# Prompt attention of a hybrid decoder in 64*64 products: query halves, key halves and identity products in place of transposes

## What is computed

```python
s_c = einsum('btgjd,bcgd->btgjc', qg, kc) - slopes * c_dist    # 63 compressed keys
p_c = masked_softmax(s_c, c_mask); o_c = einsum('btgjc,bcgd->btgjd', p_c, vc)
...  # selected: every causal block (16 of 16 are chosen); window: the last 512 keys
o = g[:, :, 0] * o_c + g[:, :, 1] * o_s + g[:, :, 2] * o_w
```

## Time and profile before

| | us |
|---|---|
| median of three runs (1698.94 to 1709.0) | 1705.83 |
| the profiled execution, its own time | 1709.87 |
| its span, first to last instruction | 1707.8 |
| PE busy over the span | 1625.1 (95%) |
| DVE, ACT, POOL busy | 874.4, 576.3, 411.4 |
| the stage `attend_prompt`: first score to last gate | 678.5 to 923.5 |
| product instructions of the stage: scores, turns, values | 512, 592, 1184 |

### The profile page before, as it was taken

How to read it: one execution, slowest core, us unless ns; L and a number is a source line. 1 busy time by engine, 2 the same in 40 slices (tenths; PEclk the granted TensorE clock), 3 DMA queues, 4 the chain that set the end, 5 groups by cost and what they waited for, 6 DMA issues and landing times. The chain is left out here.

```text
span 1707.8 us, 45233 instructions
## 1 busy us (share of the span) xinstructions
PE 1625.1 (95%) x19863; PEld 1163.6 (68%) x19863; DVE 874.4 (51%) x1780; ACT 576.3 (34%) x1239; POOL 411.4 (24%) x455
## 2 busy tenths in 40 slices
PE   7999999999999998999997989899999999999997
PEld 5788777777776555676666879665678888445443
DVE  3433555556654376777766644361141465634434
ACT  5221444444542113667663211213222211101344
POOL 0212322233331161556454210123100022100110
PEclk9999999999999999999999989899999999999999
DMA  5112010000101305802003975558601220700001
GB/s 165 37 50 56 4 28 17 16 17 16 29 16 35 93 23 117 229 40 100 1 2 106 319 221 175 170 126 190 149 21 50 80 103 16 272 0 1 25 25 50
DMA packets 116872, 136.15 MB, mean 80 GB/s; under 512 B 48620, under 2 KB 99509, under 8 KB 111726
## 3 DMA queue, kind: packets, MB, share of 16 engines
q1 hardware_dynamic: 107426, 83.97, 17.3%
q0 software_dynamic: 9216, 49.29, 9.6%
q10 hardware_dynamic: 36, 0.01, 0.0%
HBM read 120.64 MB, written 16.62 MB: 80 GB/s over the span
## 5 line engine op out<-in xcount | busy, mean ns | idle before, releaser
L1232 PE MATMUL ps<-xnT,rw_side_w 64*64 64x344 f32 x2304 | 213.6, 455 | 3.7 <-ACT zT L1557 1.9
L2672 PE MATMUL ps<-xnT,zT 128*128 128x344 f32 x384 | 121.5, 466 | 0.0
L1232 PEld LDWEIGHTS ps<-xnT,rw_side_w 64*64 64x64 f32 x2304 | 96.1, 133 | 34.6 <-issue 11.7
L2405 POOL TENSOR_SCALAR probs<-probs,row_sums,gates 128x63 f32<-128x63 f32 (+6 forms) x148 | 95.1, 658 | 100.9 <-DVE row_sums L2361 100.3
L2672 PEld LDWEIGHTS ps<-xnT,zT 128*128 128x128 f32 x384 | 72.0, 195 | 36.4 <-issue 6.3
L2310 ACT ACTIVATE probs<-probs,neg_max 128x63 f32<-128x63 f32 (+6 forms) x148 | 87.5, 595 | 1.6 <-DVE neg_max L2351 1.6
L2257 PE MATMUL ps<-kT,zT 64*128 64x512 f32 (+3 forms) x384 | 74.1, 498 | 2.3 <-PEq L82 1.4
L3379 POOL TENSOR_TENSOR mT<-mT,gate_n 128x258 f32<-128x258 f32 x28 | 23.7, 854 | 216.3 <-DVE gate_n L3342 216.3
L2284 PE MATMUL ps<-probsT,kvtok 128*64 128x128 f32 x1056 | 75.3, 280 | 0.0
L2326 ACT ACTIVATE probsT<-ps 128x512 f32<-128x512 f32 (+1 forms) x80 | 45.8, 573 | 82.3 <-PE ps L2270 82.3
L2270 PE MATMUL ps<-ident,probs 128*128 128x128 f32 (+1 forms) x460 | 68.1, 279 | 4.7 <-DVE probsT L2382 3.1
(11 more groups left out here) (623 smaller groups left out, 3613.7 us busy)
## 6 DMA issues: line engine op xcount, KB each, us to landing
w_z<-in_w_in_dram SPq DMA_DIRECT2D x13, 512.0 KB, 5.2
xnT_kept<-xnT SPq DMA_DIRECT2D x1, 4128.0 KB
x_tok<-in_x_prompt_dram SPq DMA_DIRECT2D x8, 512.0 KB
rw_side_w<-in_w_in_dram SPq DMA_DIRECT2D x16, 256.0 KB, 3.5
zT<-in_w_in_dram SPq DMA_DIRECT2D x8, 512.0 KB, 5.0
ring_k<-in_w_in_dram SPq DMA_DIRECT2D x8, 512.0 KB, 5.2
w_out<-in_w_out_dram SPq DMA_DIRECT2D x1, 4096.0 KB
h_tok<-in_x_prompt_dram SPq DMA_DIRECT2D x8, 512.0 KB, 8.6
```

Source lines behind the costliest of these rows:

```text
L1232: last = nc.tensor.matmul(k.ps[half(f), bank, 0:CG], w.side[half(e), g // 3 % 2, c, half(f)], k.xnT[half(e), c, third(g)], start=(phase == ...
L2405: nc.gpsimd.tensor_scalar(every, every, ls[:, at:at + 1], k.gates[:, i, gate:gate + 1], ALU.mult, ALU.mult).then_inc(scaled, 1)
L2672: ins = self.nc.tensor.matmul(self.k.ps[:, self.banks[n % nb], 0:CG], self.w[:, t % 2, c, :], self.k.xnT[:, c, g * CG:(g + 1) * CG], start ...
```

## The change

- Scores: each product for 128 queries becomes two for 64 queries, on the two halves of the partitions of the same bank.
- Turns: a transpose becomes four products of 64*64 with the 64*64 identity (two for the 63 compressed keys). The query half e goes to bank 4 + e, the key half f to half of the partitions. T now stands for a *group* of two pieces (84 groups, 8 of them with one piece), which fills both banks; ACT copies bank 4 and DVE bank 5, after the whole group. Turns of group u wait for both copies of group u-1, values for both copies of their group.
- Values: each product over 128 keys becomes two over 64 keys, with their sums in bank 6 and bank 7.
- The end of a unit: DVE's gate becomes `join`, which adds bank 6 and bank 7 into SBUF (a ring of four); POOL multiplies by the gate (`gated`), three units later in its order. The first values of a unit wait for the join of the unit before.
- The order: where the first of two pieces of values is a unit's last, the second one goes behind the turns, if there are any.

The core of the diff; removed lines that are printed above are left out:

```diff
@@ -2070 +2070,2 @@
-AT_RING, AT_LEAD, AT_GROUP, AT_SLOTS = 6912, 4, 4, 5
+AT_RING, AT_LEAD, AT_GROUP, AT_SLOTS = 6912, 4, 4, 3
+AT_SUMS, AT_GATE_LAG = 4, 3
...
@@ -2146 +2147,8 @@
...
+            read, turned = [("V", pc) for pc in waiting[a:a + 2]], now[a:a + 2]
+            late = len(read) == 2 and waiting[a] in self.last_piece
+            self.events += read[:1] if late else read
+            if turned:
+                self.events.append(("T", len(self.groups)))
+                self.group_of.update((pc, len(self.groups)) for pc in turned)
+                self.groups.append(turned)
+            self.events += read[1:] if late else []
@@ -2208 +2216,2 @@
-        pt = sb("probsT", [P, NPT, 512])
+        pt = sb("probsT", [P, NPT, 2, 512])
+        both = sb("both_halves", [P, AT_SUMS, P])
...
@@ -2234,0 +2244,13 @@
+        def key_halves(br):
+            return (NCMP,) if br == 0 else (HD, HD)
+
+        def copied(u, e):
+            pieces = [plan.pieces[pc] for pc in plan.groups[u]]
+            m = NCMP if all(piece[0][1] == 0 for piece in pieces) else P
+            w = 256 * (len(pieces) - 1) + 2 * HD * len(pieces[-1])
+            return pt[0:m, u % NPT, e, 0:w], k.ps[0:m, 4 + e, 0:w]
+
+        def read_before(eng, u):
+            if u >= NPT:
+                eng.wait_ge(pvd, plan.groups[u - NPT][-1] + 1)
+
@@ -2256,3 +2278,5 @@
...
+                    for f in range(2):
+                        for g in range(2):
+                            last = nc.tensor.matmul(k.ps[half(f), 2 * (s % 2) + g, at:at + w],
+                                                    k.qT[half(g), j, i * P + f * HD:i * P + (f + 1) * HD],
+                                                    keys[half(g), t0:t0 + w], start=True, stop=True)
@@ -2262,10 +2286,16 @@
...
+            def turn(u):
+                for pc in plan.groups[u]:
+                    n = plan.pieces[pc][0][0]
+                    pe.wait_ge(scaled, 6 * n + max(2 * (3, 1, 2)[br] for _, br, t in plan.pieces[pc]))
+                if u:
+                    pe.wait_ge(pt_a, u)
+                    pe.wait_ge(pt_v, u)
+                for r, pc in enumerate(plan.groups[u]):
+                    for b, (n, br, t) in enumerate(plan.pieces[pc]):
+                        for g in range(2):
+                            at = r * 256 + (2 * b + g) * HD
+                            for f, m in enumerate(key_halves(br)):
+                                for e in range(2):
+                                    last = nc.tensor.matmul(k.ps[f * HD:f * HD + m, 4 + e, at:at + HD],
+                                                            region(n, br, g, t * P + f * HD, m)[half(e)], k.ident[half(e), half(e)],
+                                                            start=True, stop=True)
@@ -2275,4 +2305,6 @@
...
+                n, u = plan.pieces[pc][0][0], plan.group_of[pc]
+                r = plan.groups[u].index(pc)
+                if pc == plan.first_of[n] and n:
+                    pe.wait_ge(joined, n)
+                pe.wait_ge(pt_a, u + 1)
+                pe.wait_ge(pt_v, u + 1)
@@ -2280,7 +2312,8 @@
...
+                    for f, m in enumerate(key_halves(br)):
+                        for g in range(2):
+                            rows, at, lo = slice(f * HD, f * HD + m), (1 + 2 * br) * P + g * HD, r * 256 + (2 * b + g) * HD
+                            vals = k.vc[rows, half(g)] if br == 0 else k.kvtok[rows, plan.first_tile(n, br) + t, at:at + HD]
+                            last = nc.tensor.matmul(k.ps[half(g), 6 + f, 0:P].rearrange("p (e q) -> p e q", e=2), vals,
+                                                    pt[rows, u % NPT, :, lo:lo + HD], start=(br == 1 and t == 0),
+                                                    stop=(br == 0 or f == 1 and br == 2 and t == plan.tiles(n, br) - 1),
+                                                    skip_group_check=True)
...
@@ -2321,2 +2349,2 @@
-                elif kind == "T" and u % 2 == 0:
-                    to, src = copied(u)
+                elif kind == "T":
+                    to, src = copied(u, 0)
@@ -2324,2 +2352 @@
-                    if u >= NPT:
-                        act.wait_ge(pvd, u - NPT + 1)
+                    read_before(act, u)
...
@@ -2363,2 +2390 @@
-            def gate(n):
-                j, i = n // NT, AT_ORDER[n % NT]
+            def join(n):
@@ -2366,2 +2392,4 @@
-                dst = k.zgn[:, j, i * P:(i + 1) * P]
-                nc.vector.tensor_tensor(dst, k.ps[:, 6 + n % 2, 0:P], dst, ALU.mult).then_inc(gatedo, 1)
+                if n >= AT_SUMS:
+                    dve.wait_ge(gatedo, n - AT_SUMS + 1)
+                nc.vector.tensor_reduce(both[:, n % AT_SUMS, :], k.ps[:, 6:8, 0:P].rearrange("p e n -> p n e"), AX.X, ALU.add
+                                        ).then_inc(joined, 1)
...
@@ -2393,0 +2421,6 @@
+            def gated(n):
+                j, i = n // NT, AT_ORDER[n % NT]
+                pool.wait_ge(joined, n + 1)
+                dst = k.zgn[:, j, i * P:(i + 1) * P]
+                nc.gpsimd.tensor_tensor(dst, both[:, n % AT_SUMS, :], dst, ALU.mult).then_inc(gatedo, 1)
+
@@ -2406,0 +2440,4 @@
+                if n >= AT_GATE_LAG:
+                    gated(n - AT_GATE_LAG)
+            for n in range(plan.N - AT_GATE_LAG, plan.N):
+                gated(n)
```

More of the change, by code:

```diff
@@ L2108, in __init__ @@
             self.last_piece.append(len(self.pieces) - 1)
-        self.events, queue, waiting = [], [], []
+        self.events, self.groups, self.group_of, queue, waiting = [], [], {}, [], []
         ready = 0
@@ L2137, in __init__ @@
             first = min(s for s, parts in enumerate(self.steps) for part in parts if part[0] == n and part[1] == br)
-            assert m is None or where["T", self.last_piece[m]] < where["S", first], (n, br, g, m)
+            assert m is None or where["T", self.group_of[self.last_piece[m]]] < where["S", first], (n, br, g, m)
     def turns(self, s, queue, waiting, ready):
@@ L2145, in turns @@
         for a in range(0, max(len(waiting), len(now)), 2):
-            self.events += [("V", pc) for pc in waiting[a:a + 2]] + [("T", pc) for pc in now[a:a + 2]]
+            read, turned = [("V", pc) for pc in waiting[a:a + 2]], now[a:a + 2]
[6 more added lines that the diff above has]
+            self.events += read[1:] if late else []
         return queue[len(now):], now, ready
@@ L2255, in score @@
                     t0 = plan.first_tile(n, br) * P + lo
-                    for g in range(2):
-                        last = nc.tensor.matmul(k.ps[:, 2 * (s % 2) + g, at:at + w], k.qT[half(g), j, i * P:(i + 1) * P],
-                                                keys[half(g), t0:t0 + w], start=True, stop=True)
+                    for f in range(2):
[3 more added lines that the diff above has]
+                                                    keys[half(g), t0:t0 + w], start=True, stop=True)
@@ L2272, in turn @@
                 last.then_inc(pt_ps, 1)
             def values(pc):
[L2275 to L2278, removed]
-                for b, (n, br, t) in enumerate(plan.pieces[pc]):
[L2280 to L2286, removed]
+                n, u = plan.pieces[pc][0][0], plan.group_of[pc]
@@ L2295, in _ @@
                     values(u)
[L2297 to L2300, removed]
         @block.scalar
@@ L2348, in mask @@
                         elif plan.freed[n, br, g] is not None:
[L2349 removed]
+                            dve.wait_ge(pt_ps, plan.group_of[plan.last_piece[plan.freed[n, br, g]]] + 1)
                         to = neg_m if final else first_m
@@ L2376, in _ @@
                         done += 1
-                elif kind == "T" and u % 2 == 1:
-                    to, src = copied(u)
+                elif kind == "T":
+                    to, src = copied(u, 1)
                     dve.wait_ge(pt_ps, u + 1)
-                    if u >= NPT:
-                        dve.wait_ge(pvd, u - NPT + 1)
+                    read_before(dve, u)
                     nc.vector.tensor_copy(to, src).then_inc(pt_v, 1)
@@ L2385, in _ @@
                     if u == plan.last_piece[n]:
-                        gate(n)
+                        join(n)
                 elif kind == "R":
```

5 lines of the change are left out of this document (2 added, 3 removed).

## The result

The changed kernel takes **1741.03 us** (median of four runs, 1733.03 to 1745.35) where the kernel before, on the same chip, takes 1706.17: a ratio of 1.020 [1.0156, 1.0244]. Slower, as forecast, but by 35 us instead of 15, and outside the range (1688 to 1734). The profiled execution has a span of 1743.6 us, 35.8 more than before. From the stage's first score to the first transfer of the next stage it went from 245.8 us to 279.0, **+33.2**; what stands in front of it is 1.4 shorter and what comes after 4.0 longer.

A forecast was written before the change was run, and what follows sets the result against it. PE was taken to bound the stage, with 30 us of excess at array shape changes to remove. New waits outweighed this: +10 +2 +1 +0.5 +1.5 = +15 us, giving 1721 us on the median, range 1688 to 1734.

The forecast's parts named there:

- The products' prices: PE's scores, turns and values: same time in 64*64 as before; identity products 14.7 ns, a turns group 0.94 us.
- the sum: Changed stage: +10 us three cycles, +2 opening, +1 last half cycle and end, +0.5 join and multiply, +1.5 feed: +15.
- Rival C: Changed stage: identity products take 18 ns, not 14.7, or the feed runs dry; 16 us, half hidden; 1729 to 1737; chance 0.08.
- The serial waits: Stage's repeating cycle: second turns wait for both copies, values for the previous unit's join; net +3.3 us a cycle.
- the eleven rounds: One repeating cycle of the changed stage, 59.5 us before; gains and losses worked round by round, together +3.3 us.
- Round j: Round of the cycle with 3.67 us of ACT exponentials: late coefficients, copy and join make it 6.3 against 4.87, loss 1.5.
- The join and POOL's multiply: End of each unit: DVE's join takes 0.35 us, bounds 0.27 and 0.69; POOL's multiply costs 0, at most 9 us.
- the instruction feed: PE in the changed stage: 7744 product instructions instead of 2288 now and then run dry; +1.5 us, bounds 0 and 8.
- A: Start of each second turns group: DVE and ACT are ready, only bare latency counts; -21 us, 1685; chance 0.27.
- rounds d and j: Rounds of the cycle where late ACT exponentials delay coefficients: 6.5 against 6.43 and 6.3 against 4.87 us.
- B: Four losing rounds of the cycle lose half of what was said; about 0 a cycle, 1706 us; chance 0.20.
- b, g, h, j: Rounds of the cycle said to lose 0.6, 0.6, 0.6 and 1.5 us to waits for copies or join.

The follow-up runs named there:

- Experiment 4: The changed kernel with turns as 128*128 transposes again, groups, waits on both copies, value halves and join kept: 1722.48 us, ratio 1.0106.
- experiment 3: The changed kernel without the stores of rows and window buffers, its early gathers issued after POOL's last unit: 1745.04 us, ratio 1.0261.
- experiment 7: The changed kernel with DVE's coefficients behind a round's first copy of turns: 1730.45 us, ratio 1.0148; same edit on the kernel before: 1702.46 us, 1.0002.
- values only: The kernel before with scores and values in 64*64, join and POOL's multiply; turns stay transposes copied piece by piece: 1700.25 us, ratio 1.0015.
- turns only: The changed kernel with whole values in 128*64 and DVE's gate, no join or POOL multiply; scores and grouped turns stay 64*64: 1725.53 us, 1.011.

## Why the prediction was right and where it failed

**The products' prices: right.** Turns in 0.95 us (0.94 said), values 0.88, scores 1.72, no excess between them. That excess was there to take: PE's busy time in a cycle fell from 58.1 to 52.0 us, 6.1 us, where the sum counts 11 x 0.68 = 7.5. Rival C's first half (identity products slower than 14.7 ns) is out.

**The serial waits: right, and so was the form of the sum.** Taking each of the eleven rounds at its shortest of three cycles:

| | a | b | c | d | e | f | g | h | i | j | k | sum |
|---|---|---|---|---|---|---|---|---|---|---|---|---|
| measured | 5.34 | 5.13 | 5.28 | 6.54 | 6.48 | 5.44 | 5.05 | 5.33 | 5.58 | 6.26 | 6.15 | 62.6 |
| said, of those with a figure | | | | 6.5 | | | 5.3 | 5.4 | 5.62 | 6.3 | 6.25 | 62.8 |

(62.8 is 59.5 + 3.3.) Round j shows the chain as it was worked out; ACT, DVE and PE in order of time:

```profile
914.41 0.60 ACT L2353 ACTIVATE probsT<-ps 128x512 f32<-128x512 f32 x1 [1.84 <-PE ps L2299]
914.91 1.03 ACT L2338 ACTIVATE kT<-kT,neg_max 128x896 f32<-128x896 f32 x1
...
918.71 0.17 DVE L2386 TENSOR_SCALAR row_sums<-row_sums 128x6 f32<-128x6 f32 x1 [1.25 <-ACT probs L2338]
...
919.03 0.53 DVE L2409 COPY probsT<-ps 128x384 f32<-128x384 f32 x1
...
919.47 0.41 DVE L2394 TENSOR_REDUCE both_halves<-ps 128x128 f32<-128x256 f32 x1
...
919.94 0.67 PE L2316 MATMUL ps<-probsT,kvtok 64*64 64x128 f32 x16 [2.20 <-DVE both_halves L2394]
```

ACT's exponentials start 0.74 us after the round (0.75 said), the coefficients at 4.54 (4.55), PE at 5.77 after the join (5.9). The chain of this round is: ACT's copy delays ACT's exponentials, these delay DVE's coefficients, these DVE's copy, this the join, and PE stands for the sum. The three cycles at their shortest rounds lose 3 x 3.1 = 9.3 us, where the sum has 10. Experiment 4, where no feed wait stands in the way, gives the whole of this part, with some excess at changes of shape in it: 15.9 us against the 10 + 2 + 1 + 0.5 = 13.5 of the sum, 11.8 in the cycles, 2.4 in the opening and 1.7 in the rest.

**The join and POOL's multiply: right in size.** The lines of the stage, the counterpart of the earlier trace rows:

```profile
L2425 POOL TENSOR_TENSOR zT<-both_halves,zT 128x128 f32<-128x128 f32 x32 | 14.7, 460 | 8.6 <-DVE both_halves L2394 8.6
L2394 DVE TENSOR_REDUCE both_halves<-ps 128x128 f32<-128x256 f32 x32 | 13.0, 408 | 2.2 <-PE ps L2316 2.2
```

The join is recorded at 0.41 us, inside the bounds 0.27 and 0.69 (0.35 taken). POOL's multiply does hold up scalings a little, since it waits 8.6 us for joins; PE's waits for POOL are 7.0 us, against 2.4 at L2270 before. No run takes this multiply away by itself, so its cost of 0 was neither shown nor refuted.

**The step that failed is the instruction feed:** "Bounds 0 and 8 us; much of it would fall into waits, so +1.5." It cost 17.3 us by experiment 4, over ten times the value taken and twice the upper bound. (That 17.3 and 15.9 add up to the 33.2 of the stage is no further evidence, since the one was got by subtracting the other. By another way, the three cycles alone took 202.6 us against 3 x 62.6 with every round at its shortest, 14.8 more.) Rival C had named the mechanism ("or the feed runs dry"), but its 16 us came from slower products, half of it hidden, and it had a chance of 0.08. Two readings were wrong. First, the bound came from the earlier trace rows alone, which is one line: over all lines that stretch of the kernel before (192 to 600 us, 11127 products, as dense as the changed stage) has 16 waits for issue, 10.4 us together. Scaled to 7744 products that is 7.2 us, about the 6.8 us that experiment 3 measured without large transfers in the cycles. So the stretch held the feed's waits without transfers beside it (it moves 29 GB/s on average, the gather 272 to 417), and nothing in the prediction stood for the rest. Second, the feed waits were thought of as lying beside other waits, and hardly any did: PE's waits for copies and joins are 29.0 us in the changed stage and 31.0 in experiment 4, so most of the 17.0 us of issue waits came on top of them. That they grow beside transfers was not in the prediction at all.

**Rivals A and B:** A needed coefficients that end ahead of the turns; rounds d and j show the opposite, and even experiment 7, which takes the coefficients out of the way, leaves the third cycle at 60.9 against 59.5. B needed half of the losses in b, g, h, j; at the shortest rounds they are 0.54, 0.40, 0.54 and 1.39 us, 2.9 of the 3.3 said.

## What to carry to other kernels

Count instructions per microsecond, not only columns (the changed stage has 27.8 products a microsecond, the one before 9.3): tiling the array four ways multiplies the instructions at equal array time, and a product that was one instruction (a transpose) became eight here. Where PE is 98% busy, taking its excess away pays only as far as the engines behind it keep their slack; give the next group of PE's work a copier that is not behind another wait (own banks and own copiers did that before), and change only the part that adds no wait, as the scores here. And read such a change in its stage and cycle by cycle: cycles of equal work and unequal time say at once that something from outside the dependencies is at work.

## What was not expected of the hardware

- **PE can run out of instructions, the more so beside large transfers.** Waits for issue and the length of the stage:

| kernel | products | issue waits of products, us | stage, us |
|---|---|---|---|
| before | 2288 | 0 | 245.8 |
| values only | 3856 | 0 | 251.0 |
| grouped transposes | 3856 | 0 | 261.7 |
| turns only | 6688 | 3.4 | 264.5 |
| after, no transfers in the cycles | 7744 | 6.8 | (end not comparable) |
| after, no stores | 7744 | 12.7 | 275.5 |
| after, late coefficients | 7744 | 16.3 | 275.1 |
| after | 7744 | 17.0 | 279.0 |
| after, late gathers | 7744 | 17.2 | 281.2 |

The page lists a queue of its own for instructions. Over the whole run (packets, MB, share of the 16 engines' time):

```profile
q8 instruction: 201, 3.29, 0.8%
```

These are packets of 16 KB; before there are 158. In the second cycle it has 15 packets after the change and 5 before, on the same 16 DMA engines as the gather. The trace has the start of each packet, and beside PE's waits it settles what "issue" is here. A packet goes with 259 records of PE on average (products and weight loads: 15809 records, 61 packets in the changed stage). The six kernels with 64*64 turns have 88 waits of products for issue in their stages, and 84 of them end 2.1 to 2.9 us after a packet began; of PE's 214 waits for other engines there, 29 do. Of the 16 in the RWKV stage of the kernel before, 15 do. The longest wait of the changed kernel ends at 734.22; its packet began at 731.80, 6.6 us after the one before. The DMA view of 731.75 to 731.85 has this line alone:

```profile
q8 instruction: 1, 0.02, 55.4%
```

The four others are among the handfuls beside the gather: no packet begins there between 810.97 and 821.84. The view of 812.2 to 821.8 has the gather's queue alone:

```profile
q0 software_dynamic: 446, 3.30, 92.3%
```

Nor does any packet in the changed stage begin less than 3.3 us after the one before it (median 4.2; before the change 8.2 at least, median 12.8). 259 records in 3.3 us are 13 ns each, while PE gets through an identity product and its weight load, two records, in 14.8 ns. So a burst uses up instructions faster than packets came in any of these runs, and lives on what has come ahead of it. Why a packet starts later beside a transfer is not shown.

- **A stall is paid twice.** In the first cycle PE stands 2.6 us for issue, and the stretch behind it has a lower granted clock (the clock falls so three times after the opening's first round, each time at a wait for issue of 1.1 us or more; at two other waits of 1.2 and 2.1 us it does not):

```profile
734.22 0.90 PE L2316 MATMUL ps<-probsT,kvtok 64*64 64x128 f32 x10 [2.60 <-issue]
734.93 1.79 PE L2299 MATMUL ps<-ident,probs 64*64 64x64 f32 x55
```
```profile
735.00:740.00 5.00, 3.90 (x130) 3.52 (x126) 1.32 (x4) 2.20 (x7) 2.72 (x5) 0.76 0.08 30
```

0.76 is a mean between the two levels, 2.4 and 1.2 GHz. The 55 identity products run from 734.93 to 736.48, 28 ns each, twice 14.8, so they ran at 1.2 GHz. This round took 8.84 us, of which 2.6 are the stall; undisturbed it takes 5.13.

A join that reads one half of a bank pair while PE writes the other half, which would take its wait away, was not tried.
